# A two-block transformer kernel on one Trainium2 core: the first four output tiles side by side, side streams on other rows, and small products joined, cut in halves or made transposes

## Chip, core and metric

The kernel runs on one core of a Trainium2 chip. The metric is the time of one launch on the device, in microseconds (us). The engines are PE (TensorE, the matrix multiplier; its weight loads are shown apart as PEld), DVE (VectorE), ACT (ScalarE), POOL (GpSimd) and SP (SyncE, which here issues loads and stores). Matrix products end in PSUM, eight banks of 128 partitions x 512 floats; everything else lives in SBUF.

## The reference, cut to what matters

512 tokens of width 1024 go through two blocks, each with two token mixers, a gated merge, an MLP and a gated embedding. Everything is float32.

```
def first_block(x, p, ...):
    u = rmsnorm(x, norm_mix_g) @ w_in
    u_rwkv, u_attn, u_gate = split(u)
    o_a = rwkv7_time_mix(u_rwkv, ...)          # recurrence over time, 8 heads of 64
    o_b = diff_attention(u_attn, ...)          # 4 heads, softmax(s0) - lam * softmax(s1), causal
    g_a, g_b = split(sigmoid(u_gate))
    x = x + (g_a * (o_a @ w_proj_a) + g_b * (o_b @ w_proj_b)) @ w_out
    x = x + square(relu(rmsnorm(x) @ w_ff1)) @ w_ff2
    return x + (p @ w_ple) * sigmoid(rmsnorm(x) @ w_ple_gate)

def second_block(x, p, ...):
    hq, hk, hv, hr, ha, hatt, hgate = split(rmsnorm(x) @ w_in)
    o = gla_mixer(hq, hk, hv, log_a)           # chunks of 64 tokens, 4 heads, dk 128, dv 256
        # attn = tril(q_dec @ k_in.T); o_intra = attn @ v; o_inter = q_dec @ state
    for g, (win, dil) in enumerate(((128, 1), (512, 4), (2048, 16))):
        o_g, lse_g = dilated_attention(...)    # 4 heads of 128, log-sum-exp of each query
    wts = softmax(stack(lses), axis=0)         # over the three groups
    o_att = sum(wts[..., None] * stack(outs), axis=0)
    x = x + (sigmoid(g_gla) * y_gla + sigmoid(g_att) * y_att) @ w_out
    ...                                        # MLP, gated embedding, final norm
```

## The kernel before

**Dense rows.** Activations lie transposed, features on partitions and tokens along the row. A product with weights is made of output tiles of 128 features, and each tile of 8 rows, one for each block of 128 of the contraction. A row is three matmuls of 128x128 on 128x512 (L571, L572, L573), since both operands are split in a high and a low part: high x high, high x low, low x high. The program has some 2,450 rows, numbered from 0 in the order of the run.

**Weights.** SP loads a tile (1024 columns a partition: 8 rows of 128) into one of four RAW buffers. ACT copies it into WHI, rounded (L1171), and DVE subtracts to get WLO (L1770). WHI and WLO have three buffers each. The work for a later tile is placed on each engine at a fixed k of a tile of now.

**Side streams.** Everything that is not a dense row is a stream of steps: "a" differential attention, "r" the RWKV preparation, "f0" and "f1" the fronts (the data of two pairs of quarters for the recurrence), "c" and "e" the recurrence itself, "g" the gated linear attention, "l" the dilated attention. weave_order() puts the steps at dense rows through put(stream, rows), by hand, and every engine walks the same order. So each engine's instructions stand in one fixed queue, and a step that waits holds all behind it on its engine.

**Rows used below.** Rows 0 to 95 are the twelve attention tiles, 96 to 207 the RWKV tiles, 208 to 335 the gates; GLA's outputs stand at rows 1130 to 1226, the end of the dilated attention at 1516 to 1600.

**The start.** Tiles 0 and 1 run skewed (tile 1 from row 7 on), the others one after the other, each with all 8 blocks of the contraction. A row k needs block k of x loaded, split by ACT (HX, L1203) and DVE (HL, L1783). The squares of x (L1220) are summed (POOL, and DVE at L1766), split again (L1229 and L1790), and summed over partitions on PE at row 24 (total, L594 and L595); ACT makes 1/rms of it, and with that DVE evicts the first tiles (L1763).

**Attention of one head.** "qk" makes scores in PSUM (L746, L747), DVE adds the bias and takes the maximum (L2156), ACT exponentiates, "aw" weights and joins both softmaxes on DVE (L2173, L2178). PE transposes the result with the identity (pt, ten L753 at row r + 21), ACT copies it out (L1480), PE multiplies by V (pv, L760), and the head's squares are summed on PE (ss, L766), from which ACT makes 1/rms (L1491) for DVE's multiplication (L1763). "vt" is the transposition of V, copied out by ACT at L1462.

**Fronts.** The first step of a front multiplies on DVE (L1763) and squares on ACT (L1520); its second step sums the squares on PE (L792), which waits for ACT. The steps after it use the norm on ACT (L1523, L1525) and DVE.

**Recurrence.** For each quarter, five levels: a "c" step on PE ("la" and "lb": products) and an "e" step on DVE, which adds the results into T and Q (L1766).

**GLA.** For each head and half vb of dv: four 128x128 products of V with the causal attention (L1063), then seven products of the chunk states with 64 queries (L1066), 128 output rows x 64 columns each.

**End of the dilated attention.** The log-sum-exps of three groups are brought from columns to rows by twelve products with the identity (L1143), turned into weights, and each is spread over 128 partitions for its head by two products with a column of EYE on 4 rows, high and low part (L1154, 24 in all).

## Time and profile before

| | |
|---|---|
| times of three runs | 1980.01, 1980.01, 1974.45 us (median 1980.01) |
| profiled execution | 1975.9 us, of which the span of the trace is 1974.1 us |
| granted TensorE clock, mean of the span | 0.994 of full speed |
| PE busy | 1933.8 us, 98% |
| DVE, ACT, POOL busy | 978.8, 777.8, 289.0 us |
| share of the chain that ended last | PE 84%, DVE 7%, ACT 4% |

The span is the time from the first to the last instruction of the profiled execution; the rest of its time, 1.8 us, lies around it. The chain is followed back from the last instruction: at each step to what released it. A busy PE is not PE at its peak: its time also hangs on the clock it is granted.

### The profile page before, as it was taken

To read this page: it belongs to the slowest core of one execution; us is meant where nothing else is said; L and a number is where in the kernel's file an instruction comes from. 1 tells how busy PE (TensorE), PEld (TensorE's weight loads), DVE (VectorE), ACT (ScalarE), POOL (GpSimd) and SP (SyncE) were. 2 spreads that over 40 slices of the span, in tenths; PEclk is the share of its full clock that TensorE was granted. 3 is DMA by queue.
4 is the path that set the end of the run, shared out by engine and by line. 5 is a ranking of instruction groups with operands and counts; after the bars stand their busy time and mean duration, and the time that the engine had idled before them with its cause. 6 is when DMAs were issued, how large, how long until landed. Compare 5 with 4: busy or idle time off the path is not lost.

```text
span 1974.1 us, 27695 instructions
## 1 busy us (share of the span) xinstructions
PE 1933.8 (98%) x11560; PEld 1576.5 (80%) x11560; DVE 978.8 (50%) x1550; ACT 777.8 (39%) x1260; POOL 289.0 (15%) x281
## 2 busy tenths in 40 slices
PE   8989999999999999999999999999999999999997
PEld 6866777778888888887787888887888888888886
DVE  6655766657432333367645344447533432333365
ACT  6555323244443332346333333344222443232345
POOL 1001233302210010122000000004201210010124
PEclk9999999999999999999999999999999999999999
DMA  5122111135233322234312122222222242223221
GB/s 198 64 69 70 66 55 61 56 123 186 82 117 118 109 96 99 93 107 136 110 54 71 68 75 86 77 84 75 96 96 95 88 150 96 98 95 102 93 94 54
DMA packets 60080, 185.70 MB, mean 94 GB/s; under 512 B 6595, under 2 KB 11843, under 8 KB 59828
## 3 DMA queue, kind: packets, MB, share of 16 engines
q1 hardware_dynamic: 59956, 183.94, 27.7%
q8 instruction: 91, 1.49, 0.3%
q14 instruction: 33, 0.27, 0.0%
HBM read 173.69 MB, written 10.22 MB: 93 GB/s over the span
## 4 chain that ended last, share of the span: by engine, by line
PE 84%; DVE 7%; ACT 4%; issue 2%; POOL 2%; DMA 1%; SPq 0%; DVEq 0%; POOLq 0%; ACTq 0%
PE P L571 25%; PE P L573 24%; PE P L572 24%; DVE AREN L1763 2%; POOL AREN L2497 1%; DVE AREN L1766 1%; DVE WLO L1770 1%; ACT WHI L1171 1%; ACT AREN L1475 1%; PE P L1100 1%; PE P L1066 1%; PE P L760 1%; PE P L907 1%; PE P L919 0%; PE P L923 0%
## 5 line engine op out<-in xcount | busy, mean ns | idle before, releaser
L571 PE MATMUL P<-HH,WHI 128*128 128x512 f32 x1528 | 614.3, 402 | 5.3 <-DVE HL L1783 3.4
L573 PE MATMUL P<-HH,WLO 128*128 128x512 f32 x1528 | 597.6, 391 | 0.0
L572 PE MATMUL P<-HL,WHI 128*128 128x512 f32 x1528 | 596.9, 391 | 0.0
L1171 ACT ACTIVATE WHI<-RAW 128x1024 fp32r<-128x1024 f32 x302 | 318.1, 1054 | 432.5 <-PE P L573 431.6
L1770 DVE TENSOR_TENSOR WLO<-RAW,WHI 128x1024 fp32r<-128x1024 f32 x302 | 376.7, 1248 | 146.2 <-ACT WHI L1171 144.7
L571 PE MATMUL P<-ARR,WHI 128*128 128x512 f32 (+1 forms) x920 | 353.3, 384 | 0.0
L572 PE MATMUL P<-ARR,WHI 128*128 128x512 f32 (+1 forms) x920 | 352.8, 384 | 0.0
L573 PE MATMUL P<-ARR,WLO 128*128 128x512 f32 (+1 forms) x920 | 352.8, 384 | 0.0
L571 PEld LDWEIGHTS P<-HH,WHI 128*128 128x128 f32 x1528 | 287.8, 188 | 77.3 <-issue 7.9
L573 PEld LDWEIGHTS P<-HH,WLO 128*128 128x128 f32 x1528 | 287.6, 188 | 61.9
L572 PEld LDWEIGHTS P<-HL,WHI 128*128 128x128 f32 x1528 | 288.2, 189 | 55.8 <-issue 0.2
L2497 POOL TENSOR_TENSOR AREN<-AREN 128x512 f32<-128x512 f32 (+1 forms) x121 | 136.6, 1136 | 1109.3 <-ACT AREN L1440 551.9
L571 PEld LDWEIGHTS P<-ARR,WHI 128*128 128x128 f32 x920 | 172.9, 188 | 34.9 <-DVE AREN L1763 0.4
L573 PEld LDWEIGHTS P<-ARR,WLO 128*128 128x128 f32 x920 | 172.9, 188 | 34.1
L572 PEld LDWEIGHTS P<-ARR,WHI 128*128 128x128 f32 x920 | 172.9, 188 | 33.8
L1763 DVE TENSOR_TENSOR AREN<-P,RS 128x512 f32<-128x512 f32 (+1 forms) x138 | 102.5, 744 | 193.4 <-PE P L573 182.5
L1766 DVE TENSOR_TENSOR AREN<-AREN,P 128x256 f32<-128x256 f32 (+2 forms) x168 | 77.1, 494 | 184.3 <-PE P L573 148.9
L2500 POOL TENSOR_TENSOR AREN<-AREN 128x512 f32<-128x512 f32 (+1 forms) x66 | 105.9, 1604 | 421.7 <-DVE AREN L1763 181.9
L2099 DVE TENSOR_TENSOR ARR<-AREN,ARR 128x512 fp32r<-128x512 f32 x64 | 44.3, 692 | 226.6 <-POOL AREN L2497 210.0
L1440 ACT ACTIVATE AREN<-P 128x512 f32<-128x512 f32 x64 | 38.3, 598 | 200.2 <-PE P L573 200.2
L1763 DVE TENSOR_TENSOR AREN<-AREN 128x256 f32<-128x256 f32 (+3 forms) x78 | 44.5, 594 | 26.5 <-ACT AREN L1491 11.5
L1763 DVE TENSOR_TENSOR AREN<-P,AREN 128x512 f32<-128x512 f32 (+1 forms) x61 | 38.7, 651 | 36.8 <-PE P L573 22.5
(311 smaller groups left out, 1444.2 us busy)
## 6 DMA issues: line engine op xcount, KB each, us to landing
RAW<-in_w_in_dram SPq DMA_DIRECT2D x117, 512.0 KB, 3.3
RAW<-in_w_ff_dram SPq DMA_DIRECT2D x64, 512.0 KB, 3.3
RAW<-in_w_ml_dram SPq DMA_DIRECT2D x64, 512.0 KB, 3.3
RAW<-in_w_out_dram SPq DMA_DIRECT2D x16, 512.0 KB, 3.3
RAW<-in_w_pg_dram SPq DMA_DIRECT2D x16, 512.0 KB, 3.3
AREN<-in_xT_dram SPq DMA_DIRECT2D x16, 256.0 KB, 6.0
s_gates<-AREN SPq DMA_DIRECT2D x16, 256.0 KB, 2.0
RAW<-in_w_ab_dram SPq DMA_DIRECT2D x8, 512.0 KB, 3.3
```

Of the source, the lines that this page charges most:

```text
L571: e.matmul(out, hi, H[0][:, s], start=first, stop=False)
L572: e.matmul(out, hi, H[1][:, s], start=False, stop=False)
L573: return e.matmul(out, lo, H[0][:, s], start=False, stop=last)
L760: d = e.matmul(bank(b)[:, 128 * kb:512], VT[:, 128 * kb:128 * kb + 128], PTD[:, KOF[kb]:KOF[kb] + 512 - 128 * kb], start=kb == 0, stop=kb ...
L1171: e.activation(WHI[n % NSPL][:, :], RAW[n % NRAW][:, :], ACT.Copy).then_inc(*D.act.sig("whi", n))
L1440: e.activation(r, bank((0, 1, 2, 3)[j % 4]), ACT.Relu).then_inc(*D.act.sig(H1, q, j))
L1763: return e.tensor_tensor(out, a, b, ALU.mult)
L1766: return e.tensor_tensor(out, a, b, ALU.add)
L1770: e.tensor_tensor(WLO[n % NSPL][:, :], RAW[n % NRAW][:, :], WHI[n % NSPL][:, :].bitcast(F32), ALU.subtract).then_inc(*D.dve.sig("wlo", n))
L2099: e.tensor_tensor(HD[j][1], ar(19 + u % 3), HD[j][0].bitcast(F32), ALU.subtract).then_inc(*D.dve.sig(f + "D", q, j))
L2497: return e.tensor_tensor(out, a, b, ALU.mult)
L2500: return e.tensor_tensor(out, a, b, ALU.add)
```

## The change

It touches seven places.

**1. The start.** The first four tiles run side by side: for each block k, rows of the tiles 0 to 3 in the banks 0, 1, 6 and 7. Their weights come from four new weight tiles, w_lead, each with two blocks k for all four tiles. The second half of the first weight tile and the next two are loaded earlier between the blocks of x, ACT's squares stand between the HX instructions, and the total stands at row 23.

**2. The attention stream.** It starts at row 34 (32), head 0 at row 40 (39), and the step ss of the head before stands behind aw (row r + 12) where it stood in r + 3.

**3. The fronts.** Front 0 has rows 182, 189, 192, 194 (174, 178, 181, 184), front 1 196, 200, 203, 205 (196, 199, 202, 205).

**4. The recurrence.** DVE's additions into Q of the levels 1 to 4 move from the step "la" to "lb", with the order T of both pairs, then Q of both.

**5. GLA.** Each of the seven products with 128 output rows and 64 columns becomes two with 64 output rows, written to the upper and lower half of the bank's partitions; both vb stand in one step.

**6. Log-sum-exp.** The twelve products with the identity become transposes.

**7. Mixing weights.** The high part lies on partitions 0 to 3 and the low part on 96 to 99 of one buffer, zero between them (three memsets on POOL); EYE has ones at both places, and one product on 100 rows takes the place of two on 4.

The diff, cut:

```diff
+def lead4(n):
+
+    for k in range(8):
+        for j in range(4):
+            yield j, k
+    for j in range(4, n):
+        for k in range(8):
+            yield j, k
...
-            out += [("pv", h - 1, 0)] if h and i == 1 else [("ss", h - 1, 0)] if h and i == 5 else []
+            out += [("pv", h - 1, 0)] if h and i == 1 else []
             out.append(("qk", h, i))
         out.append(("aw", h, 0))
+        out += [("ss", h - 1, 0)] if h else []
         out += [("vt", h + 1, 0)] if h < 3 else []
...
-        late = r > 39
-        put("a", r, r, r, *((r,) if late else ()), r + 3, r + 3, r + 3, *((r + 3,) if late else ()), r + 6, r + 6,
-            r + 11, *((r + 13,) if r < 117 else ()), r + 21, r + 21, r + 21, r + 21)
+    put("a", 34)
+    for r in (40, 65, 91, 117):
+        late = r > 40
+        put("a", r, r, r, *((r,) if late else ()), r + 3, r + 3, r + 3, r + 6, r + 6, r + 11,
+            *((r + 12,) if late else ()), *((r + 13,) if r < 117 else ()), r + 21, r + 21, r + 21, r + 21)
     put("a", 142, 148)
     put("r", 149, 153, 153, 156, 156, 160, 160, 164, 164, 168)
 
-    for jj, rows in ((0, (174, 178, 181, 184)), (1, (196, 199, 202, 205))):
+    for jj, rows in ((0, (182, 189, 192, 194)), (1, (196, 200, 203, 205))):
         put(f"f{jj}", *rows)
...
 
-                g = units(("attn",), T_AT, lead2(12, 6), H1, hx("HX"), ev("attn"), (0, 1, 6, 7))
-                for j, k in lead2(12, 6):
-                    if (j, k) == (3, 0):
-                        total("n1", 2)
-                    next(g)
-                    yield
+                for k in range(8):
+                    for j, b in enumerate((0, 1, 6, 7)):
+                        if (j, k) == (3, 5):
+                            total("n1", 2)
+                        w.wait_ge(D.dve.at("wlo", k // 2) if k else D.dve.at("wlo0"), D.dve.at("HX", k))
+                        d = row(bank(b), k // 2, 4 * (k % 2) + j, H1[k], k == 0, k == 7)
+                        if k == 7:
+                            d.then_inc(*D.pe.sig("attn", j))
+                            free[b] = D.dve.at("attn", j)
+                        elif j == 3 and k % 2:
+                            d.then_inc(*D.pe.sig("lead", k // 2))
+                        yield
+                yield from units(("attn",), T_AT, ((j, k) for j in range(4, 12) for k in range(8)), H1, hx("HX"),
+                                 ev("attn"), (0, 1, 6, 7))
...
                         yield
+                    w.wait_ge(G.dve.at("at", h, 1), G.dve.at("s", h, 7), free.get(4), free.get(5))
                     for vb in range(2):
-                        cs = slice(128 * vb, 128 * vb + 128)
-                        b = 4 + vb
-                        o = bank(b)
-                        w.wait_ge(G.dve.at("at", h, 1), G.dve.at("s", h, 7), free.get(b))
                         for tb in range(4):
-                            e.matmul(o[:, 128 * tb:128 * tb + 128], gVT[:, tb, cs], gATv[:, tb, :], start=tb == 0,
-                                     stop=False)
+                            e.matmul(bank(4 + vb)[:, 128 * tb:128 * tb + 128], gVT[:, tb, 128 * vb:128 * vb + 128],
+                                     gATv[:, tb, :], start=tb == 0, stop=False)
+                    for vb in range(2):
                         for c in range(1, 8):
-                            d = e.matmul(o[:, 64 * c:64 * c + 64], gST[:, c, cs], q[:, 64 * c:64 * c + 64],
-                                         start=False, stop=c == 7)
+                            for x, rw in enumerate(rws):
+                                d = e.matmul(bank(4 + vb)[rw, 64 * c:64 * c + 64],
+                                             gST[:, c, 128 * vb + 64 * x:128 * vb + 64 * x + 64],
+                                             q[:, 64 * c:64 * c + 64], start=False, stop=c == 7)
                         d.then_inc(*G.pe.sig("o", h, vb))
-                        free[b] = G.dve.at("o", h, vb)
-                        yield
+                        free[4 + vb] = G.dve.at("o", h, vb)
+                    yield
+                    yield
...
-                        d = e.matmul(o[0:4, 128 * qb:128 * qb + 128], LSE[:, 16 * g + 4 * qb:16 * g + 4 * qb + 4],
-                                     ident, start=True, stop=True)
+                        d = e.transpose(o[0:4, 128 * qb:128 * qb + 128], LSE[:, 16 * g + 4 * qb:16 * g + 4 * qb + 4], ident)
                     d.then_inc(*L.pe.sig("l", g))
                     free[b] = L.act.at("l", g)
...
-                        b, o = take(L.dve.at("ls", g), K.pool.at("eye"))
-                        for i_ in range(2):
-                            d = e.matmul(o, EYE[0:4, h:h + 1].to_broadcast([4, 128]), dLS[g][i_], start=i_ == 0,
-                                         stop=i_ == 1)
-                        d.then_inc(*L.pe.sig("mix", h, g))
+                        b, o = take(L.dve.at("ls", g), K.pool.at("eye", 1))
+                        e.matmul(o, EYE[0:100, h:h + 1].to_broadcast([100, 128]), arr(28 + g)[0:100, :], start=True,
+                                 stop=True).then_inc(*L.pe.sig("mix", h, g))
                         free[b] = L.dve.at("mix", h, g)
...
-                    if j == 5:
+                    if j == 0:
+                        w.wait_ge(raw(0))
+                        e.activation(WHI[0][:, 512:1024], RAW[0][:, 512:1024], ACT.Copy).then_inc(*D.act.sig("whi", 0))
+                    else:
+                        square1(j - 1)
+                    if j == 1:
                         whi(1)
                     if j == 3:
-                        w.wait_ge(raw(0))
-                        e.activation(WHI[0][:, 512:1024], RAW[0][:, 512:1024], ACT.Copy).then_inc(*D.act.sig("whi", 0))
-                for j in range(2):
-                    square1(j)
+                        whi(2)
+                square1(7)
...
+                    if what == "lb" and lev < 5:
+                        add(Qm, Qm, o0[:, 128:384]).then_inc(*C.dve.sig("Q", q, lev))
...
                             add(hj(Tm), hj(Tm), both(b0, 64, 64)).then_inc(*C.dve.sig("T", q, lev))
-                        add(Qm, Qm, o0[:, 128:384] if lev < 5 else o0[:, 0:256]).then_inc(*C.dve.sig("Q", q, lev))
+                        else:
+                            add(Qm, Qm, o0[:, 0:256]).then_inc(*C.dve.sig("Q", q, 5))
...
+                w.wait_ge(L.pe.at("pv", 11), L.act.at("pt", 11, 0))
+                for g in range(3):
+                    e.memset(arr(28 + g).bitcast(F32), 0.0).then_inc(*L.pool.sig("lz", g))
...
-                    if j == 5:
-                        weights(1)
-                    if j == 3:
                         load("raw0", 0, RAW[0][:, 512:1024], A[name][i, :, 512:1024])
-                weights(2)
+                    if j in (1, 3):
+                        weights((j + 1) // 2)
                 weights(3)
```

On ACT at the start, before: the squares (L1220) stand behind all the blocks of x (L1203), the copies of weight tile 0 (second half, L1215), 1, 2 and 3 (L1171) between them.

```order
L1215 ACTIVATE WHI<-RAW 128x512 [waits d_raw0]
L1203 ACTIVATE HH<-AREN,VEC 128x512 [waits d_x4]
L1203 ACTIVATE HH<-AREN,VEC 128x512 [waits d_x5]
L1171 ACTIVATE WHI<-RAW 128x1024 [waits d_raw1]
L1203 ACTIVATE HH<-AREN,VEC 128x512 [waits d_x6]
L1203 ACTIVATE HH<-AREN,VEC 128x512 [waits d_x7]
L1220 ACTIVATE AREN<-AREN 128x512 x2
L1171 ACTIVATE WHI<-RAW 128x1024 [waits d_raw2]
L1220 ACTIVATE AREN<-AREN 128x512 x6
L1171 ACTIVATE WHI<-RAW 128x1024 [waits dense_pe,d_raw3]
```

After, from behind the first block on: L1230 is the HX instruction, L1250 the square, L1240 and L1198 the weight copies.

```order
L1240 ACTIVATE WHI<-RAW 128x512 [waits d_raw0]
L1230 ACTIVATE HH<-AREN,VEC 128x512 [waits d_x1]
L1250 ACTIVATE AREN<-AREN 128x512
L1198 ACTIVATE WHI<-RAW 128x1024 [waits d_raw1]
L1230 ACTIVATE HH<-AREN,VEC 128x512 [waits d_x2]
L1250 ACTIVATE AREN<-AREN 128x512
L1230 ACTIVATE HH<-AREN,VEC 128x512 [waits d_x3]
L1250 ACTIVATE AREN<-AREN 128x512
L1198 ACTIVATE WHI<-RAW 128x1024 [waits d_raw2]
L1230 ACTIVATE HH<-AREN,VEC 128x512 [waits d_x4]
L1250 ACTIVATE AREN<-AREN 128x512
L1230 ACTIVATE HH<-AREN,VEC 128x512 [waits d_x5]
```

The second half of weight tile 0 has moved from behind x3 to behind x0, tile 1 from behind x5 to behind x1, tile 2 from behind x7 to behind x3, and each square stands one block behind its HX instruction.

On DVE in the attention of head 2, before: the first row is the multiplication in the norm of head 1, which waits for ACT, and the scores (L2156) of head 2 stand behind it.

```order
L1763 TENSOR_TENSOR AREN<-AREN 128x512 [waits attn_act]
L2156 ISA AREN,SML<-P,AREN 128x256 [waits attn_pe]
L2156 ISA SML 128x1
L2156 ISA AREN,SML<-P,AREN 128x384 [waits attn_pe]
L2156 ISA SML 128x1
L2156 ISA AREN,SML<-P,AREN 128x512 [waits attn_pe]
L2156 ISA SML 128x1
L2162 TENSOR_SCALAR SML<-SML 128x4 [waits attn_dve]
L1763 TENSOR_TENSOR AREN<-P,RS 128x512 [waits dense_pe]
```

After, the same stretch and its end, where the multiplication (L1792, waits for attn_act) now stands:

```order
L2186 ISA AREN,SML<-P,AREN 128x256 [waits attn_pe]
L2186 ISA SML 128x1
L2186 ISA AREN,SML<-P,AREN 128x384 [waits attn_pe]
L2186 ISA SML 128x1
L2186 ISA AREN,SML<-P,AREN 128x512 [waits attn_pe]
L2186 ISA SML 128x1
L2192 TENSOR_SCALAR SML<-SML 128x4 [waits attn_dve]
...
L2208 SCALAR_TENSOR_TENSOR AREN<-AREN,SML 128x384 [waits attn_dve]
L2208 SCALAR_TENSOR_TENSOR AREN<-AREN,SML 128x512 [waits attn_dve]
L1792 TENSOR_TENSOR AREN<-AREN 128x512 [waits attn_act]
L2171 TENSOR_SCALAR AREN<-CST 128x512
L2176 TENSOR_TENSOR ARR<-AREN,ARR 64x512 [waits attn_act]
```

The multiplication has moved past the scores and the weighting of head 2, up to the split for the transposes of V of head 3.

On ACT at the first front, before: L1520 is the square that L792 waits for; in front of it stands a weight copy.

```order
L1171 ACTIVATE WHI<-RAW 128x1024 [waits dense_pe,d_raw3]
L1520 ACTIVATE AREN<-AREN 128x256 [waits front0_dve]
L1242 ACTIVATE AREN<-AREN,DVC 128x512 [waits dense_dve]
L1171 ACTIVATE WHI<-RAW 128x1024 [waits dense_pe,d_raw0]
L1523 ACTIVATE AREN<-AREN 128x256 [waits front0_dve]
L1525 ACTIVATE AREN<-AREN 128x256 [waits front0_act]
L1242 ACTIVATE AREN<-AREN,DVC 128x512 [waits dense_dve]
```

After: L1549 is the same square.

```order
L1198 ACTIVATE WHI<-RAW 128x1024 [waits dense_pe,d_raw3]
L1271 ACTIVATE AREN<-AREN,DVC 128x512 [waits dense_dve]
L1198 ACTIVATE WHI<-RAW 128x1024 [waits dense_pe,d_raw0]
L1549 ACTIVATE AREN<-AREN 128x256 [waits front0_dve]
L1271 ACTIVATE AREN<-AREN,DVC 128x512 [waits dense_dve]
L1198 ACTIVATE WHI<-RAW 128x1024 [waits dense_pe,d_raw1]
L1552 ACTIVATE AREN<-AREN 128x256 [waits front0_dve]
L1554 ACTIVATE AREN<-AREN 128x256 [waits front0_act]
L1271 ACTIVATE AREN<-AREN,DVC 128x512 [waits dense_dve]
```

The square has moved behind one gate instruction (L1242, now L1271) and one more weight copy, eight dense rows later.

## Rows read from the trace of the kernel before

**Rows 1.** Busy time of each engine, page.

```profile
PE 1933.8 (98%) x11560; PEld 1576.5 (80%) x11560; DVE 978.8 (50%) x1550; ACT 777.8 (39%) x1260; POOL 289.0 (15%) x281
```

**Rows 2.** Window in the attention: span, busy PE, PEld, DVE, ACT, POOL; clock, DMA.

```profile
115.00:120.00 5.00, 2.66 (x5) 1.47 (x6) 2.72 (x4) 2.97 (x6) 0.00 (x0) 0.55 0.31 108
```

**Rows 3.** PE at the start: start us, us, operation, [idle before].

```profile
6.28 0.57 PE L571 MATMUL P<-HH,WHI 128*128 128x512 f32 x1
...
14.99 0.50 PE L571 MATMUL P<-HH,WHI 128*128 128x512 f32 x1 [1.69 <-DVE HL L1783]
...
27.40 0.39 PE L594 MATMUL P<-ARR,ONES 128*128 128x512 f32 x1
...
33.11 0.39 PE L573 MATMUL P<-HH,WLO 128*128 128x512 f32 x1
```

**Rows 4.** ACT at the start, same columns.

```profile
6.20 0.72 ACT L1203 ACTIVATE HH<-AREN,VEC 128x512 fp32r<-128x512 f32 x1 [0.85 <-DMA AREN<-in_xT_dram]
8.01 1.40 ACT L1203 ACTIVATE HH<-AREN,VEC 128x512 fp32r<-128x512 f32 x2 [1.08 <-DMA AREN<-in_xT_dram]
...
11.96 1.06 ACT L1171 ACTIVATE WHI<-RAW 128x1024 fp32r<-128x1024 f32 x1 [0.57 <-DMA RAW<-in_w_in_dram]
...
16.14 3.22 ACT L1220 ACTIVATE AREN<-AREN 128x512 f32<-128x512 f32 x6
```

**Rows 5.** DVE at the start, same columns.

```profile
23.89 0.68 DVE L1790 TENSOR_TENSOR ARR<-AREN,ARR 128x512 fp32r<-128x512 f32 x1
```

**Rows 6.** DVE in the attention of head 2, same columns.

```profile
96.58 0.69 DVE L1763 TENSOR_TENSOR AREN<-AREN 128x512 f32<-128x512 f32 x1 [3.40 <-ACT AREN L1491]
```

**Rows 7.** PE at head 2's transposes and head 3's first scores, same columns.

```profile
107.63 0.88 PE L753 MATMUL P<-CST,AREN 128*128 128x128 f32 x6 [0.66 <-DVE AREN L2178]
109.47 0.66 PE L753 MATMUL P<-CST,AREN 128*128 128x128 f32 x4 [0.97 <-ACT AREN L1462]
...
116.95 0.45 PE L746 MATMUL P<-ARR 128*128 128x128 f32 x1 [3.38 <-ACT AREN L1480]
```

**Rows 8.** Waits of PE: line and releaser: us in total, times, longest.

```profile
PE P L760 <- ACT AREN L1480: 1.2, 2, 0.9
```

**Rows 9.** PE at the first front, same columns.

```profile
182.12 1.22 PE L792 MATMUL P<-AREN,CST 128*128 128x256 f32 x2 [3.89 <-ACT AREN L1520]
182.77 0.99 PE L571 MATMUL P<-HH,WHI 128*128 128x512 f32 x1
...
187.79 0.40 PE L571 MATMUL P<-HH,WHI 128*128 128x512 f32 x1
```

**Rows 10.** DVE at the first front, same columns.

```profile
180.06 1.23 DVE L1770 TENSOR_TENSOR WLO<-RAW,WHI 128x1024 fp32r<-128x1024 f32 x1 [6.36 <-ACT WHI L1171]
```

**Rows 11.** Chain that ended last, recurrence and GLA: start us, us, piece.

```profile
229.91 1.33 DVE AREN L1766 x4
...
254.69 1.08 PE P L874 x32
...
988.83 1.51 PE P L1066 x14
```

**Rows 12.** PE, a product of the recurrence with its shape, same columns as rows 3.

```profile
254.62 1.15 PE L874 MATMUL P<-AREN 128*64 128x64 f32 x32
```

**Rows 13.** PE at the end of the dilated attention, same columns.

```profile
1327.22 1.91 PE L1143 MATMUL P<-CST,SML 128*4 128x128 f32 x16 [0.16 <-ACT AREN L1723]
...
1364.33 0.39 PE L573 MATMUL P<-HH,WLO 128*128 128x512 f32 x1
1364.65 1.79 PE L1154 MATMUL P<-ARR,EYE 4*128 4x512 f32 x6
...
1368.84 0.63 PE L572 MATMUL P<-HL,WHI 128*128 128x512 f32 x1
```

**Rows 14.** PE at the last mixing weights, same columns.

```profile
1375.28 1.32 PE L1154 MATMUL P<-ARR,EYE 4*128 4x512 f32 x4 [0.42 <-DVE AREN L1763]
```

**Rows 15.** DVE at the last mixing weights, same columns.

```profile
1374.54 1.88 DVE L1763 TENSOR_TENSOR AREN<-P,AREN 128x512 f32<-128x512 f32 x3
```

75 lines of the change are left out of this document (43 added, 32 removed).

## The prediction

> **What bounds the kernel now.** The first view is the table of the profile page on busy time: PE is busy 1933.8 us of the span of 1974.1 us, 98%, and the next engine, DVE, half of it [rows 1]. So the reader looks for two things only: work that leaves PE, and the 40 us in which PE stands still or runs slowly. The second view is the windows: between 115 and 120 us PE's granted clock is 0.55 of full speed [rows 2], which is about the lower of the two levels (1.2 of 2.4 GHz). The third is PE's timeline around such places, and then that of ACT and DVE, which say why PE waited. A dense row costs 0.69 us: from the matmul at 14.99 to the total at 27.40 PE runs 54 matmuls [rows 3], 0.23 us each. Seven edits, seven terms; anything hidden behind PE is worth nothing.
>
> **1. The start: -0.7.** Before, PE runs the 18 matmuls of six rows between 6.28 and 14.99, 8.71 us [rows 3]; by the rate above they need 4.1, so 4.6 us are waits for blocks of x. After, each block feeds four rows, 2.76 us of work, and PE waits little for blocks. Block 0 ends at 6.28 + 2.76 = 9.0. Behind the second half of weight tile 0, block 1 lands where the third load landed, 8.0 (its ACT instruction waits for it, [rows 4]); with an ACT split of 0.70 and a DVE split as long it is ready at 9.5. Nineteen more rows bring PE to the total at 9.5 + 13.1 = 22.6. But the total needs the sum of squares. Weight tile 1 landed at 11.96 behind four more pieces, 1.5 MB in the 4 us since 8.01 [rows 4]; now only it follows block 1, so it lands at about 8.0 + 1.3 = 9.3. ACT then has two weight copies (1.04), six HX (0.70 at most, 0.66 mean) and seven squares (3.22 / 6 = 0.54) [rows 4] in a row: 2.1 + 4.0 + 3.8 = 9.9, to 19.2. Weight copy 3 ends at 20.2, its DVE half at 21.4, because DVE now takes WLO of tile 3 ahead of the sums. Four sums at 0.68 (the time of the like-sized split L1790, [rows 5]) end at 24.1, WLO of tile 4 at 25.3, L1790 at 26.0. So PE waits 3.4 us at the total, which had no wait before [rows 3]. Total (0.46) and nine rows (6.2) end at 32.7; before, row 31 ended at 33.11 + 0.23 = 33.3 [rows 3]. Ends: -4.1, if the sums are ready in time, and +1.9, if the wait of 3.4 also halves the clock for the next four rows (2.6 more, priced in part 3).
>
> **2. Attention: -2.5.** DVE waits 3.40 us for the norm factor of the head before at 96.58, with the scores of the present head behind it in the queue [rows 6]. Moved behind the weighting, this multiplication leaves the scores 3.40 + 0.61 earlier, and the weighting (L2178) too. PE waited for it 0.66 us, then 0.97 for a bank [rows 7]; both go, and so does the 0.9 at the last product with V [rows 8]: 2.5. What I leave is the 3.38 at 116.95, where head 3's first scores wait for a copy of ACT [rows 7]: it follows PE's own transposes by as much as now. What is late next is the "ss" itself, but its result is wanted one head later. Ends: -1 (the copies of weights on ACT hold the exponentials) and -5.9 (the 3.38 goes too).
>
> **3. Front 0: -4.2.** PE waits 3.89 at 182.12 for ACT's square [rows 9]; DVE had been idle 6.36 us for a weight copy, and the front's first multiplication stands behind that [rows 10]. The step now sits eight rows (5.5 us) later and its consumer seven rows behind it, so this wait goes. After it PE's matmuls run at half clock: the four rows from 182.77 to 187.79 took 5.02 us, 2.3 more than 12 x 0.23, and L792 itself some 0.3. All together 6.5. Against it, DVE and ACT now do front 0 while front 1 keeps its place two rows behind it, at 196, with the consumer at row 200. By my count of the two queues the square of front 1 is some 2 us late there, so 2.3 is given back. Ends: -2.0 and -6.5.
>
> **4. Recurrence: +0.5.** The additions into Q run beside products already. Four T and Q pieces take 1.33 us [rows 11], 0.33 each; the new order delays Q of the first pair by one T, 0.33, where DVE is the last to come. At 16 levels the worst is 16 x 0.33 = +5.3, but PE has dense rows between the levels (98% busy), so I take one or two of them. The lower end is 0.
>
> **5. GLA: -3.7.** Seven products take 14 passes (each float32 product is two) and 1.51 us, 0.108 a pass [rows 11]. After, 28 passes of 64 output rows. The nearest row is L874 of the recurrence, 32 passes of just such a shape (128*64, 128x64) [rows 12], which alternate between the column halves: 1.08 us, 0.034 each [rows 11]. So 28 x 0.034 = 0.95 instead of 1.51, 0.56 less, times 8 (four heads, two vb) = -4.5. For entering and leaving this form I take eight times 0.1, the 0.09 by which L1154 starts behind the matmul at 1364.33 + 0.23 [rows 13]: -3.7. Ends: -1.0 (0.09 a pass with some of the pairs overlapped) and -4.5.
> The Trainium skill, TensorEngine Tiling (Array Packing), Key Properties, says that a change of the tiling mode drains TensorE, and under Restrictions that column tiling rules out fast weight load. Taken as one drain at each product it would make this edit a loss; the rows of L874, where halves alternate without a gap, speak against that reading, and one drain at each end is within the 0.8 above.
>
> **6 and 7. End of the dilated attention: -3.3.** The first twelve products are recorded as 24 passes, 16 of them in 1.91 us, 0.12 each [rows 13]; a transpose is one pass, so -1.4. The mixing weights lose 12 of 24 products at 0.23, -2.8, and as each group of three now holds PE for half as long, half of the switches, -0.7. Behind the first group the matmuls ran at 0.63 where they are 0.39 elsewhere [rows 13]; seven at the half-clock rate of part 3 (5.02 / 12 = 0.42) cost 1.4. Together -6.3. But DVE takes 0.63 for each multiplication with a mixing weight (1.88 for three, [rows 15]), more than PE's 0.23, and PE already waits 0.42 for a bank from it [rows 14]. With half of the work PE only waits longer for banks; I give back 3.0. The three memsets are on POOL, which is 85% idle [rows 1]. Ends: -1.4 and -6.3.
>
> **Sum.** -0.7 - 2.5 - 4.2 + 0.5 - 3.7 - 3.3 = -13.9, from the profiled execution's 1975.9: 1962.0. That execution lies 4.1 below the median of the three runs, 2.3 below their mean (1978.2); I add half of the latter: **1963.0**. A measurement of this kernel can tell about 0.3%, 5.9 us, from no change.
>
> **Rivals.**
> *The waits come back (0.17).* Every wait at the start and the fronts has ACT and DVE behind it, not PE. If they are as late at the new rows: start +1.5, attention -1.0, front -2.6, recurrence +0.5, GLA -3.7, mixing -1.3, sum -6.6: 1970. For it: the 6.36 at 180.06 [rows 10] is a wait for a weight copy, which any row has. Against it: the consumer of front 0 has seven rows where it had four.
> *All of it lands (0.16).* Half of the start's wait is not there (-1.7), the half clock at 115 to 120 goes with an earlier ACT (-2.6, from [rows 2]), mixing keeps its 3.0 (DVE's banks are free): -13.9 - 7.3 = -21.2, less some overlap 1956.
> *Nothing to be seen (0.06).* Earlier side streams only shift which queue is late; three terms of seven, -3 to -5 in all: 1973 to 1976.
> *Slower (0.05).* The column halves of GLA don't overlap, and each of the 112 alternations pays a switch: 224 passes at 0.108 instead of 112 are +12.1, 112 x 0.1 more +11.2; with the other terms at -10.2 that is +13: about 1990. It decides from 0.1 us a pass on, where the edit costs the 10.2 that the others bring. L874 at 0.034 speaks against it [rows 11, 12]; for it, its products each start anew, while these add into one bank behind others of the full width.
> *Forecast (0.56).* 1957 to 1968 around 1963.
>
> **The numbers.** Down to 1954 the range takes in the case in which all lands, up to 1973 the one in which the waits come back; what is left out is the last two rivals and the far ends. Faster by over 0.3%: 0.56 + 0.16 + most of 0.17 = 0.86; within: the third rival and the rest, 0.09; slower 0.05.
>
> **What the changed profile would show.** Right: PE waits some 3 us at the total (L594's new line) at 23 us and nowhere else ahead of it; no wait of DVE over 3 us in head 2; no 3.9 at row 180, but some 2 us at row 200; the seven products of each vb in 0.9 to 1.0 us; the transposes in half of their time; clock 1.0 behind the first mixing group, with waits of 0.3 to 0.5 for banks in the later ones. Wrong: half clock behind the total or at row 200, GLA passes over 0.1, a wait of PE at the recurrence's levels after Q, or a new wait of POOL at the memsets that holds its additions.

## The result and the profile after

The changed kernel takes 1962.19 us (median of four runs, 1960.48 to 1962.56), the kernel before in the same session 1978.48 (four runs, 1974.45 to 1980.01). The ratio is 0.9919, with a 95% interval of 0.9902 to 0.9937: faster by 0.8%. The profiled execution takes 1960.48 us and its span is 1958.7, 15.4 less than the 1974.1 before.

The first view is again the page's table of busy time, here of the changed kernel.

```profile
PE 1921.4 (98%) x11648; PEld 1569.2 (80%) x11648; DVE 981.7 (50%) x1550; ACT 777.4 (40%) x1260; POOL 293.0 (15%) x286
```

To be read against [rows 1]: PE is 12.4 us less busy and as dominant as before (98%). So the bound has not changed, and 3.0 of the 15.4 are waits of PE that went.

Where the time went is best read by dense rows, since both kernels run the same ones. The table is worked out from PE's timeline of both kernels: the first line is the time at which row 32 starts, each other line the time from the first matmul of one dense row to that of another.

| dense rows | what stands there | before, us | changed, us | gain | forecast |
|---|---|---|---|---|---|
| up to 32 | start | 34.26 | 33.99 | -0.3 | -0.7 |
| 32 to 150 | attention | 119.18 | 114.99 | -4.2 | -2.5 |
| 150 to 208 | RWKV preparation, fronts | 54.61 | 50.50 | -4.1 | -4.2 |
| 208 to 384 | recurrence | 253.90 | 254.97 | +1.1 | +0.5 |
| 384 to 1120 | nothing changed | 509.05 | 509.05 | 0 | 0 |
| 1120 to 1248 | GLA | 135.12 | 130.54 | -4.6 | -3.7 |
| 1512 to 1520 | log-sum-exp | 9.62 | 8.54 | -1.1 | |
| 1560 to 1600 | mixing weights | 37.43 | 35.22 | -2.2 | -3.3 for both |
| 1600 to 2400 | nothing changed | 545.01 | 545.01 | 0 | 0 |

The gains add up to -15.4, all of the span's difference. The stages in which nothing changed agree to 0.01 us over 545, so such a table can show a few tenths even where whole times differ by more between runs. That holds where PE waits little: stages with a long wait differ between runs of the same code as well (last section).

One thing in the first two lines is only moved. Before, the first step of the attention lay ahead of row 32, and took 0.92 us with its wait:

```profile
33.87 0.63 PE L737 MATMUL P<-CST,AREN 128*128 128x128 f32 x4 [0.38 <-issue]
```

Now it lies behind row 33 and takes 0.4. So row 31 ends at 33.34 before and at 33.99 in the changed kernel: the start alone is 0.65 longer, and the attention alone 4.5 shorter.

**Start.** PE's timeline, then DVE's and POOL's, of the changed kernel; columns as in [rows 3].

```profile
9.39 0.47 PE L594 MATMUL P<-HH,WHI 128*128 128x512 f32 x1
...
25.70 0.47 PE L615 MATMUL P<-ARR,ONES 128*128 128x512 f32 x1 [2.84 <-DVE ARR L1819]
...
28.42 0.63 PE L594 MATMUL P<-HH,WHI 128*128 128x512 f32 x1
```

```profile
13.64 2.32 DVE L1799 TENSOR_TENSOR WLO<-RAW,WHI 128x1024 fp32r<-128x1024 f32 x1
...
19.61 1.21 DVE L1799 TENSOR_TENSOR WLO<-RAW,WHI 128x1024 fp32r<-128x1024 f32 x1
20.75 3.07 DVE L1795 TENSOR_TENSOR AREN<-AREN 128x512 f32<-128x512 f32 x4
23.74 1.22 DVE L1799 TENSOR_TENSOR WLO<-RAW,WHI 128x1024 fp32r<-128x1024 f32 x1
24.88 0.68 DVE L1819 TENSOR_TENSOR ARR<-AREN,ARR 128x512 fp32r<-128x512 f32 x1
```

```profile
11.30 5.82 POOL L2533 TENSOR_TENSOR AREN<-AREN 128x512 f32<-128x512 f32 x3 [5.91 <-ACT AREN L1250]
```

The second block starts at 9.39 (9.5 in the forecast), and the 4.6 us of waits for blocks of x [rows 3] are down to tenths. Then PE waits 2.84 us at the total at 25.70 (3.4 at 26.0 in the forecast), and matmuls of 0.63 behind it show half clock. Ahead of the total DVE runs the low part of a weight tile (19.61), the four sums, another weight tile, and L1819: the chain of the forecast.

**Attention and fronts.** PE's timeline of the changed kernel.

```profile
106.45 1.25 PE L782 MATMUL P<-CST,AREN 128*128 128x128 f32 x10
...
114.04 0.30 PE L775 MATMUL P<-ARR 128*128 128x128 f32 x1 [2.91 <-ACT AREN L1509]
...
115.09 4.11 PE L789 MATMUL P<-AREN 128*128 128x512 f32 x8 [0.64 <-ACT AREN L1509]
...
173.60 0.39 PE L594 MATMUL P<-HH,WHI 128*128 128x512 f32 x1
...
191.41 0.70 PE L821 MATMUL P<-AREN,CST 128*128 128x256 f32 x2 [1.96 <-ACT AREN L1549]
```

Head 2's ten transposes (106.45) have no wait, where 0.66 and 0.97 stood in [rows 7]. The wait for ACT's copy is still there, 2.91 where it was 3.38. Dense row 178, at 173.60, starts without the 3.89 of [rows 9] and at full clock. The wait of front 1 at row 200 (L821, 191.41) is 1.96, which the forecast had put at "some 2".

**GLA and the end of the dilated attention.** Groups of PE by line, count, busy us and mean ns, first of the kernel before and then of the changed one.

```profile
L1066 PE MATMUL P<-AREN 128*128 128x64 f32 x112 | 13.4, 271 | 0.0
...
L1154 PE MATMUL P<-ARR,EYE 4*128 4x512 f32 x24 | 7.1, 419 | 0.4 <-DVE AREN L1763 0.4
...
L1143 PE MATMUL P<-CST,SML 128*4 128x128 f32 x24 | 2.9, 272 | 0.2 <-ACT AREN L1723 0.2
```

```profile
L1094 PE MATMUL P<-AREN 128*64 128x64 f32 x224 | 7.4, 224 | 0.0
...
L1182 PE MATMUL P<-ARR,EYE 100*128 100x512 f32 x12 | 4.3, 424 | 1.6 <-DVE AREN L1792 0.9 <-DVE ARR L2501 0.6
...
L1173 PE MATMUL P<-CST,SML 128*4 128x128 f32 x12 | 1.6, 272 | 0.7 <-ACT AREN L1752 0.7
```

```profile
982.15 1.85 PE L1094 MATMUL P<-AREN 128*64 128x64 f32 x56
...
1315.14 1.04 PE L1173 MATMUL P<-CST,SML 128*4 128x128 f32 x8 [0.69 <-ACT AREN L1752]
...
1351.38 0.63 PE L1182 MATMUL P<-ARR,EYE 100*128 100x512 f32 x2
1352.64 0.50 PE L1182 MATMUL P<-ARR,EYE 100*128 100x512 f32 x1 [0.62 <-DVE ARR L2501]
1353.89 0.50 PE L594 MATMUL P<-HH,WHI 128*128 128x512 f32 x1 [0.75 <-DVE WLO L1799]
...
1362.34 1.09 PE L1182 MATMUL P<-ARR,EYE 100*128 100x512 f32 x2 [0.86 <-DVE AREN L1792]
```

The seven products of a vb cost 13.4 us before and 7.4 now: 56 passes of both vb in 1.85 us, 0.033 each. L1182 has half the passes of L1154 and takes 2.8 us less, L1173 half of L1143's and 1.3 less. Against that the waits grew: 0.69, 0.62, 0.75 and 0.86 in these rows, 2.9 together, where [rows 13, 14] have 0.16 and 0.42 and the matmul behind the first head waits 0.41 for a weight tile, 1.0 together:

```profile
1366.84 0.50 PE L571 MATMUL P<-HH,WHI 128*128 128x512 f32 x1 [0.41 <-DVE WLO L1770]
```

### The profile page after: what moved, and what is told of

Same layout as the page of the kernel before. It is cut to its first block, busy times and chain, and to the rows that moved or that the text cites. A ratio compares the mean times of both kernels' runs of the same rounds, so it can differ in the third digit from the quotient of the medians.

```text
span 1958.7 us, 27882 instructions
## 1 busy us (share of the span) xinstructions
PE 1921.4 (98%) x11648; PEld 1569.2 (80%) x11648; DVE 981.7 (50%) x1550; ACT 777.4 (40%) x1260; POOL 293.0 (15%) x286
## 4 chain that ended last, share of the span: by engine, by line
PE 84%; DVE 7%; ACT 3%; issue 2%; POOL 2%; DMA 1%; SPq 0%; DVEq 0%; POOLq 0%; ACTq 0%
PE P L594 25%; PE P L596 24%; PE P L595 24%; DVE AREN L1792 2%; POOL AREN L2530 1%; DVE AREN L1795 1%; DVE WLO L1799 1%; ACT WHI L1198 1%; PE P L1130 1%; PE P L936 1%; PE P L789 1%; DVE HL L1812 1%; PE P L948 1%; PE P L952 1%; POOL AREN L2533 0%
## 5 line engine op out<-in xcount | busy, mean ns | idle before, releaser
L1198 ACT ACTIVATE WHI<-RAW 128x1024 fp32r<-128x1024 f32 x302 | 318.0, 1054 | 433.7 <-PE P L596 432.7
L1799 DVE TENSOR_TENSOR WLO<-RAW,WHI 128x1024 fp32r<-128x1024 f32 x302 | 377.5, 1251 | 143.4 <-ACT WHI L1198 141.8
L1792 DVE TENSOR_TENSOR AREN<-P,RS 128x512 f32<-128x512 f32 (+1 forms) x138 | 102.6, 744 | 185.0 <-PE P L596 174.3
L1792 DVE TENSOR_TENSOR AREN<-P,AREN 128x512 f32<-128x512 f32 (+1 forms) x61 | 38.7, 651 | 35.8 <-PE P L596 21.1
L1792 DVE TENSOR_TENSOR AREN<-AREN 128x256 f32<-128x256 f32 (+3 forms) x78 | 44.5, 593 | 16.3 <-ACT AREN L1404 5.2
```

Of the source, the lines that this page charges most:

```text
L1198: e.activation(WHI[n % NSPL][:, :], RAW[n % NRAW][:, :], ACT.Copy).then_inc(*D.act.sig("whi", n))
L1792: return e.tensor_tensor(out, a, b, ALU.mult)
L1799: e.tensor_tensor(WLO[n % NSPL][:, :], RAW[n % NRAW][:, :], WHI[n % NSPL][:, :].bitcast(F32), ALU.subtract).then_inc(*D.dve.sig("wlo", n))
```

## Experiments

Each changes one thing in the changed kernel, unless said otherwise. All but the last were run once, with a profile; they are read by the same stages as above. Where a stage has no edit it mostly repeats to some hundredths. The five stages that hold long waits do not: the start, the attention, the fronts, the recurrence and the mixing weights (last section). So a span says little about an edit, and the stage with the edit is read.

**GLA, full width.** Both vb in one step as changed, but products with 128 output rows again:

```diff
-                            for x, rw in enumerate(rws):
-                                d = e.matmul(bank(4 + vb)[rw, 64 * c:64 * c + 64],
-                                             gST[:, c, 128 * vb + 64 * x:128 * vb + 64 * x + 64],
-                                             q[:, 64 * c:64 * c + 64], start=False, stop=c == 7)
+                            d = e.matmul(bank(4 + vb)[:, 64 * c:64 * c + 64], gST[:, c, 128 * vb:128 * vb + 128],
+                                         q[:, 64 * c:64 * c + 64], start=False, stop=c == 7)
```

> The changed kernel with GLA's outputs in one step for both vb as it is, but each of the seven products again 128 output rows wide. If the gain of 4.6 us in GLA (four steps of 1.15 us in the trace of the changed kernel) comes from the column halves, each vb takes 14 passes at 0.108 us, 1.51 us, again, all of the 4.6 us come back and the span is 1958.7 + 4.6 = 1963.3 us. Rival: the gain comes from joining both vb in one step, with one change of form where there were two; then the passes are shorter than 0.108 here as well, or the step is, and the span stays within 1 us of 1958.7.

Rows 1120 to 1248 take 135.12 us, to the hundredth what they took before. So the halves gave all of the 4.6, and joining both vb nothing. (The span is 1966.2, 7.5 more: the other 2.9 lie at the start, 1.2, and at rows 1560 to 1600, 1.7, where nothing was edited.)

**GLA, halves without alternation.**

```diff
-                        for c in range(1, 8):
-                            for x, rw in enumerate(rws):
+                        for x, rw in enumerate(rws):
+                            for c in range(1, 8):
```

> The changed kernel with GLA's column halves in another order: for each vb first all seven products of the upper half, then all seven of the lower. Theory A, the halves gain because a product in one half overlaps the one in the other half: in a row of products in the same half nothing overlaps, passes cost 0.1 us or more, and the 224 passes take some 24 us instead of 7.4, a span of about 1975 us. Theory B, the pass of 64 output rows is short by itself (fewer columns of weights to load): passes stay at 0.033 to 0.04 us and the span at 1958.7 within 1 us. Between the two, half of it is the loading of 64 columns: passes at 0.06, +5 us.

PE's timeline of head 0 in the two runs, full width first, then halves one after the other:

```profile
983.23 3.24 PE L1093 MATMUL P<-AREN 128*128 128x64 f32 x28
```

```profile
985.22 2.94 PE L1094 MATMUL P<-AREN 128*64 128x64 f32 x56
```

A pass of half width in the same half as the last one takes 2.94 / 56 = 0.052 us, half of the 0.108 of a full one (in the first row 3.24 less its end is 28 of them). The same 56 passes in alternation take 1.85 (982.15 above). By the starts of single records the picture is sharper: a full pass starts every 0.112 us, a half pass behind one in the same half every 0.058, and in alternation the two halves of a pair start 0.007 apart, a pair every 0.058. Rows 1120 to 1248 are 134.82 us: without alternation only 0.3 of the 4.6 is left. (The span is 1967.7, 9.0 more than changed; besides these 4.3, rows 32 to 150 took 1.3 more, rows 150 to 208 1.6 and rows 1560 to 1600 1.7, all without an edit.) So half width halves a pass and doubles their number, and the gain is the overlap of the two halves. Theory A is right on the mechanism and wrong on the price (0.1 and 24 us expected); the value between, 0.06, was nearest. That the halves overlap is what the Trainium skill, TensorEngine Tiling (Array Packing), says under Key Properties, that different tiles can load weights and multiply in parallel. The drain that it names there for a change of mode shows nowhere between the passes. At the two ends of the form the trace does show a cost. The first half pass starts 0.205 behind the last product of full width (0.111 in the run with full width), the second pair 0.100 behind the first (0.058 later on), and the next dense matmul 0.151 behind the last pass (0.084). That is 0.2 us a head and 0.8 for the four.

**The total four rows later**, at row 27 (the expectation calls it row 26, and three rows).

```diff
-                        if (j, k) == (3, 5):
+                        if (j, k) == (3, 6):
                             total("n1", 2)
```

> The changed kernel with the total of the first norm three rows later, at row 26, after the sum is ready. The wait of 2.84 us at 25.70 shrinks to under 0.8, since PE does three more rows (2.1 us) first, and the slow matmuls behind it (1.4 us in all against the kernel before) go. 1/rms is wanted at row 32 for the first eviction and is ready by 28.5, so nothing new waits: row 32 at 33.99 - 2.1 - 1.4 = 30.5 us, span 1955.2. Rival: the first eviction takes the place of the total, since DVE's evictions come behind a weight tile: row 32 waits, and under 1 us is won.

```profile
25.64 0.47 PE L615 MATMUL P<-ARR,ONES 128*128 128x512 f32 x1 [0.16 <-DVE ARR L1819]
...
30.73 0.47 PE L594 MATMUL P<-HH,WHI 128*128 128x512 f32 x1 [0.98 <-DVE AREN L1792]
```

The wait at the total is 0.16, and row 32 starts at 30.73, 3.3 earlier. At row 32 a wait of 0.98 for the first eviction has come, part of the rival: on DVE a weight tile stands ahead of that eviction. In nine kernels with the changed kernel's start row 32 lies between 32.0 and 35.2 (last section), so the edit is worth 1.3 at least. The span is 1959.4 all the same, 0.7 more than the changed kernel's: rows 208 to 384 and 1560 to 1600, without an edit, took 2.6 and 1.4 longer (last section).

**Front 1 later.**

```diff
-    for jj, rows in ((0, (182, 189, 192, 194)), (1, (196, 200, 203, 205))):
+    for jj, rows in ((0, (182, 189, 192, 194)), (1, (196, 202, 204, 206))):
```

> The changed kernel with the later steps of front 1 at the rows 202, 204 and 206 instead of 200, 203 and 205. The wait of 1.96 us at 191.41 for ACT's square is 2 rows, 1.4 us, shorter: 0.6 or less. Nothing else changes, and the span is 1958.7 - 1.4 = 1957.3 us. Rival: the fronts' remainder is now late for the first level of the recurrence behind row 208, and what is won at row 200 is lost there: span within 0.3 us of 1958.7.

```profile
189.09 0.70 PE L821 MATMUL P<-AREN,CST 128*128 128x256 f32 x2 [0.59 <-ACT AREN L1549]
...
195.63 1.16 PE L919 MATMUL P<-AREN 64*128 64x128 f32 x16 [0.64 <-DVE AREN L1792]
```

The wait is 0.59, as expected, but a new one of 0.64 stands in the recurrence's first products, for DVE, and rows 150 to 208 take 50.06 instead of 50.50: 0.4 of the 1.4. It is the rival, for two thirds. The span of 1955.9 is 2.8 less than changed, but 2.0 of that lie ahead of row 32, where nothing was edited.

**Additions into Q back in la.**

```diff
-                    if what == "lb" and lev < 5:
-                        add(Qm, Qm, o0[:, 128:384]).then_inc(*C.dve.sig("Q", q, lev))
...
-                        else:
-                            add(Qm, Qm, o0[:, 0:256]).then_inc(*C.dve.sig("Q", q, 5))
+                        add(Qm, Qm, o0[:, 128:384] if lev < 5 else o0[:, 0:256]).then_inc(*C.dve.sig("Q", q, lev))
```

> The changed kernel with the additions into Q back in the step la. Between the dense rows 224 and 384 the changed kernel loses 0.9 us against the kernel before (it is 8.4 us ahead at row 224 and 7.5 at row 384). If the later additions into Q cause this, the recurrence is 0.9 us shorter here, 0.3 of it at each of three levels. Rival: the 0.9 comes from the weight copies that stand beside the levels, at other rows against PE since the fronts moved: then rows 224 to 384 take as long as in the changed kernel, within 0.2 us.

```profile
313.76 0.69 PE L936 MATMUL P<-AREN 64*64 64x64 f32 x32
...
315.17 0.58 PE L594 MATMUL P<-HH,WHI 128*128 128x512 f32 x1
```

```profile
315.98 0.79 PE L936 MATMUL P<-AREN 64*64 64x64 f32 x32
...
317.48 0.58 PE L594 MATMUL P<-HH,WHI 128*128 128x512 f32 x1
```

The first two rows are of this run, the other two of the changed kernel at the same level. The dense row ahead of the level starts at 312.87 and 314.95, so the level is over after 2.30 us here and after 2.53 in the changed kernel. It is 0.23 shorter at three levels (behind rows 274, 308 and 315), as the expectation has it, with 0.23 for its 0.3. Not every level gains: at an earlier one the changed kernel waits 1.12 us in one piece and this run 0.78 and 0.20 in two, and both are over after the same time. Rows 208 to 352 take 230.59 us instead of 231.35, so 0.76 of the 0.92 that the changed kernel lost there (230.43 before) is this edit; of the remaining 0.16, 0.13 lie ahead of row 211, and their cause is open. The span of 1955.8 is 2.9 less than changed, of which 1.8 lie ahead of row 32, without an edit.

**The step ss back at row r + 3.**

```diff
-            out += [("pv", h - 1, 0)] if h and i == 1 else []
+            out += [("pv", h - 1, 0)] if h and i == 1 else [("ss", h - 1, 0)] if h and i == 5 else []
...
-        out += [("ss", h - 1, 0)] if h else []
```

> The changed kernel with the step ss of the attention back at row r + 3, the other attention rows as changed. If the attention's gain of 4.4 us between the rows 64 and 128 comes from this step, DVE waits 3.4 us for 1/rms of the head before again, PE waits 0.7 and 1.0 us at head 2's transposes and 0.9 at the last product with V, and rows 64 to 144 take 3 to 4 us longer than in the changed kernel. Rival: it is the shift of the stream's first rows (34 and 40) that gives the gain; then these rows stay within 0.5 us.

```profile
107.30 0.88 PE L781 MATMUL P<-CST,AREN 128*128 128x128 f32 x6 [0.66 <-DVE AREN L2207]
109.14 0.66 PE L781 MATMUL P<-CST,AREN 128*128 128x128 f32 x4 [0.96 <-ACT AREN L1490]
...
116.61 0.30 PE L774 MATMUL P<-ARR 128*128 128x128 f32 x1 [3.41 <-ACT AREN L1508]
...
143.97 2.42 PE L788 MATMUL P<-AREN 128*128 128x512 f32 x8 [0.86 <-ACT AREN L1508]
```

All waits of [rows 7, 8] are back, 0.66, 0.96, 3.41 and 0.86. Rows 32 to 150 take 119.06 us, 4.1 more than changed, against a gain of 4.2: this step is the attention's gain, the shift of the first rows is not. On DVE the four waits for 1/rms (L1491 before) are back as well, 3.4 the longest.

**One mixing group per dense row.**

```diff
-        *[A_HR + r for r in (72, 80, 88, 96) for _ in range(3)], A_HR + 104)
+        *[A_HR + r + i for r in (74, 80, 88, 96) for i in range(3)], A_HR + 104)
```

> The changed kernel with the mixing weights one group per dense row: rows 74, 75, 76 behind 1496 for the first head (72 before) and r, r + 1, r + 2 with r = 80, 88, 96 for the others. The changed kernel waits at the first head 0.62 us for DVE's low part and then 0.75 for a weight tile, and at the second 0.86 for a bank. If DVE's order of work causes these waits, the 0.62 and the 0.86 go, with or without the half clock behind them (1 us): rows 1560 to 1600 take 1.5 to 2.5 us less. Rival: DVE is behind as a whole here, and the waits go to the weight tiles instead: less than 0.5 us.

```profile
1356.85 0.50 PE L594 MATMUL P<-HH,WHI 128*128 128x512 f32 x1 [2.36 <-DVE WLO L1799]
```

The waits of 0.62 and 0.86 are gone, but 2.36 for a weight tile stand where 0.75 did. Rows 1560 to 1600 take 34.48 us, 0.74 less than changed, and 2.4 less than the 36.9 that most runs with the changed order take there (last section): both in part. DVE is behind as a whole, as the rival has it, but the wait at the second head was one of order.

**Two products on 4 rows for each mixing weight, transposes kept.**

```diff
-                        e.matmul(o, EYE[0:100, h:h + 1].to_broadcast([100, 128]), arr(28 + g)[0:100, :], start=True,
-                                 stop=True).then_inc(*L.pe.sig("mix", h, g))
+                        for i_ in range(2):
+                            d = e.matmul(o, EYE[0:4, h:h + 1].to_broadcast([4, 128]), dLS[g][i_], start=i_ == 0,
+                                         stop=i_ == 1)
+                        d.then_inc(*L.pe.sig("mix", h, g))
```

> The changed kernel with two products on 4 rows for each mixing weight, as before, and the transposes kept. By the count of products it is 12 x 0.23 = 2.8 us longer. By the traces of before and changed, rows 1560 to 1600 gained 2.2 us only, since waits of DVE grew from 0.8 to 2.2: so 2.2 longer here, with the waits back at 0.8. Rival: switches between 4-row and 128-row products cost as well (the 0.7 of the forecast): 3 us or more.

PE's timeline of the fourth head in this run; the changed kernel has there 3 passes in 0.87 us (1368.73 above, the third head, reads the same).

```profile
1381.19 1.65 PE L1183 MATMUL P<-ARR,EYE 4*128 4x512 f32 x6
```

At the third and fourth head nothing waits, and the 16 dense rows with the two heads take 14.45 us here and 12.44 in the changed kernel: 1.0 for each head's three groups, where three products less are 0.7. So the rival has the price: 0.3 a head is for changes between the narrow product and the dense ones. The starts of single records say the same: at each change the two next starts are 0.32 and 0.33 us apart where they are 0.23 to 0.24 elsewhere. Over four heads the edit is worth 4.0. Rows 1560 to 1600 take 39.08 us, 3.9 more than changed. Against the runs in which the same stage of the changed code took 36.9 (last section) it would be 2.2, so the whole stage alone would not decide it; the two undisturbed heads do.

**DVE's low part of weight tile 4 behind L1819.**

```diff
-                    for n in due4(j, k, 3):
+                    for n in due4(j, k, 3) if j > 3 else [n for n, r in ((3, 11), (4, 22), (5, 27)) if 4 * k + j == r]:
                         wlo(n)
```

> The changed kernel with DVE's low part of weight tile 4 three dense rows later, behind the low part of the sum of squares (L1819). By the forecast of the start the chain to the total is ACT's copies and squares, tile 3's low part, four sums, tile 4's low part and L1819, one after the other on DVE. If so, the total starts 1.14 us earlier than 25.7 (less the 0.6 in which L1819 waits for ACT's rounded sum): about 25.0, and PE's wait falls from 2.84 to 2.2. Rival: the sum is late on ACT or POOL, and the order on DVE doesn't matter: 25.7 and 2.8 as before.

```profile
25.43 0.47 PE L615 MATMUL P<-ARR,ONES 128*128 128x512 f32 x1 [2.50 <-DVE ARR L1819]
```

```profile
20.82 3.08 DVE L1795 TENSOR_TENSOR AREN<-AREN 128x512 f32<-128x512 f32 x4
24.59 0.69 DVE L1819 TENSOR_TENSOR ARR<-AREN,ARR 128x512 fp32r<-128x512 f32 x1 [0.69 <-ACT ARR L1258]
25.20 1.22 DVE L1799 TENSOR_TENSOR WLO<-RAW,WHI 128x1024 fp32r<-128x1024 f32 x1
```

L1819 now waits 0.69 for ACT's rounded sum, and starts 3.77 us behind the start of the sums; in the changed kernel it was 4.13 (20.75 to 24.88). So the chain runs over DVE as forecast, but the edit is worth 0.36, not 0.7, and the wait at the total, 2.50, is no less than the 2.53 of the next run, which has the changed kernel's order there.

**Fronts at their rows before.**

```diff
-    for jj, rows in ((0, (182, 189, 192, 194)), (1, (196, 200, 203, 205))):
+    for jj, rows in ((0, (174, 178, 181, 184)), (1, (196, 199, 202, 205))):
```

> The changed kernel with the fronts at their rows before. Rows 176 to 208 took 31.35 us before and take 27.24 in the changed kernel. If the front rows alone do that, they take 31.3 here, with PE's wait of 3.9 us at row 178 and half clock behind it, and the wait of 1.96 at row 200 goes. Rival: the other edits (earlier attention, the start) would have shortened the wait anyway: 29 to 30 us.

```profile
177.65 1.22 PE L821 MATMUL P<-AREN,CST 128*128 128x256 f32 x2 [3.89 <-ACT AREN L1549]
```

The wait of 3.89 is back to the hundredth, and rows 150 to 208 take 55.00 us (54.61 before, 50.50 changed). The rows alone did it. Being earlier with the attention doesn't help here: DVE is idle 6.35 us again, for a weight copy at 174.52, which stands on ACT behind a table load (1.28) and eight operations of the RWKV preparation (0.62 each).

**All that paid, in one kernel**: the total at row 27, tile 4's low part behind L1819 and tile 5's at row 30, behind the first eviction, front 1 at 202, 204, 206, Q back, and the mixing groups of the last three heads one per row. Beside the diffs above:

```diff
+                    for n in due4(j, k, 3) if j > 3 else [n for n, r in ((3, 11), (4, 22), (5, 30)) if 4 * k + j == r]:
...
+        *[A_HR + r + i * (r > 72) for r in (72, 80, 88, 96) for i in range(3)], A_HR + 104)
```

> The changed kernel with what the runs so far show to pay: total of the norm at row 27, DVE's low part of weight tile 4 behind the sum and of tile 5 behind the first eviction, front 1's later steps at 202, 204, 206, the additions into Q back in the step la, and the mixing groups of the last three heads one per row. By the stages of the single runs: start -3.2 and another -1.0 from DVE's order, front -0.4, recurrence -0.8, mixing -0.7, together -6.1 against the changed kernel's 1958.7: a span of about 1952.6 and 0.988 of the time before. Rival: earlier work only moves PE's half-clock stretches and its waits for weight tiles, as at the rows 356 and 1570 of the runs so far, and up to 3 us of it are lost again: 1955.5.

The span is 1954.4, between the two. Five runs give 1955.79 us (1953.43 to 1958.11) against 1976.53 for the kernel before (nine runs), a ratio of 0.9891, interval 0.9874 to 0.9909. The interval overlaps that of the changed kernel (0.9902 to 0.9937) at its edge, and the two were not timed side by side, so that it beats the changed kernel is likely by stages and not shown by times. By stages: row 32 starts at 29.91 (4.1 earlier than changed), rows 32 to 150 +0.3, rows 150 to 208 -0.4, rows 208 to 384 -0.6, rows 1560 to 1600 +0.6 with a wait of 1.75 at the second head. Of the expected 6.1 us 1.8 are missing: 1.3 at the mixing weights, 0.3 in the attention, 0.2 in the recurrence, and nearly nothing at the start (4.1 for 4.2).

## Why the prediction came true, step by step

The forecast was 1963.0 with a span near 1960, and the result 1962.19. The sum of -13.9 was 1.5 short of the -15.4 measured, and the errors of its terms go both ways.

1. *Start, -0.7.* The table has -0.3, but by the forecast's own measure, the end of row 31, it is +0.65 (33.34 to 33.99), and +0.5 as the mean of nine kernels with this start (33.8). So this term had the wrong sign. The wait at the total was 2.84 for 3.4, since ACT had copied tile 3 by 19.3 and not 20.2. What it lacked is the half clock behind the wait, which the forecast kept for its upper bound: rows 24 to 28 took 4.13 us for 2.72. Moving the total took both away. The moved first step of the attention gave 0.6 that no term had.
2. *Attention, -2.5.* Measured -4.2, or -4.5 without the first step, which now lies in this stage; the term that was most mis-sized. Row 112 with head 2's transposes is 2.1 shorter (1.6 forecast), the last product with V 1.1 (0.9): the matmuls behind a wait are slower too, and that goes with it. Row 117, which the forecast left as it was, is 0.9 shorter, 0.5 of it from the wait (3.38 to 2.91) and 0.5 from L760 behind it (4.57 to 4.11, 115.09 above). Row 86 gives 0.4, and the moved first step takes 0.4 at row 34.
3. *Fronts, -4.2.* Measured -4.1, with 6.3 gained (6.5 in the forecast) and 2.2 given back at row 200 (2.3). The forecast counted the queues for the latter; the trace adds a cause. DVE's weight tile takes 1.64 us at 188.51 and its small operations 0.83 to 0.95 at 190 where they take 1.23 and 0.42 in [rows 10] and elsewhere, while POOL multiplies. ACT's square waits for the first of the small ones. Together the tile and that operation are 0.8 longer than elsewhere, of PE's wait of 1.96:

```profile
188.51 1.64 DVE L1799 TENSOR_TENSOR WLO<-RAW,WHI 128x1024 fp32r<-128x1024 f32 x1
190.07 0.83 DVE L1792 TENSOR_TENSOR AREN<-AREN,VEC 128x256 f32<-128x256 f32 x1
190.83 0.95 DVE L2233 SCALAR_TENSOR_TENSOR AREN<-AREN,VEC 128x256 f32<-128x256 f32 x1
```

```profile
188.01 3.48 POOL L2530 TENSOR_TENSOR AREN<-AREN 128x256 f32<-128x256 f32 x3 [12.52 <-DVE AREN L1792]
```

```profile
190.94 0.42 ACT L1549 ACTIVATE AREN<-AREN 128x256 f32<-128x256 f32 x1 [3.03 <-DVE AREN L1792]
```

4. *Recurrence, +0.5.* +1.1 measured over rows 208 to 384, 0.76 of it by the edit. The term was small in both; "one or two levels" were at least two.
5. *GLA, -3.7.* -4.6 measured. The pass of L874, 0.034, was the right row: 0.033 by the same count. The 0.8 for changes of form is there too, as 0.2 for each of four heads (second experiment). What was mis-sized is the price of the passes: by the starts of records the halves save 5.5 us and not 4.5, since a full pass is 0.112 and not 0.108, and a pair of halves 0.058 and not twice 0.034.
6. *Log-sum-exp and mixing, -3.3.* -3.3 measured, as -1.1 and -2.2. The products are worth 1.3 and 4.0 (the forecast: 1.4 and 3.5), and the waits took 1.9 (2.9 for 1.0) where it had 3.0; but the half clock behind the first head, for which it had counted 1.4 as gained, stayed (1353.89 and the rows behind it). Errors that cancel.

Of the signs that the forecast named, half clock behind the total was to show it wrong, and came; clock 1.0 behind the first mixing group was to show it right, and didn't. Of the rivals, "the waits come back" was nearer at the start (+1.5) and wrong on attention and fronts. The slower one fell with GLA's 0.033 a pass. So the mechanisms of attention, fronts and GLA are right, and that the end of the sum is off by only 1.5 and the time by 0.8 is partly luck. The errors of the terms are +1.3 (start), -0.6 (the moved step), -2.0 (attention), +0.6 (recurrence) and -0.9 (GLA), which cancel in part. What was added for the one execution of 1975.9, from which the sum was made, and what the sum lacked cancelled as well.

## What to carry to other kernels

Where one engine is 98% busy, compare two traces by the start of the same unit of its work, stage by stage: terms of 0.3 us can be read where whole times differ by 5, as long as no long wait lies in the stage. Products of 64 output rows gained here only where the neighbour in the queue wrote the other half; put such products in pairs, alternating. When a step is late in another engine's queue, move its consumer, but count what both engines then do at the next consumer: three of the four steps moved here (front 0, front 1 and the total) gave back a third or more of their gain there.
